# An eleventh expert tile is kept in h, the gathers read x, and the experts' sum is collected beside x

## What is computed

```python
for l in range(DEPTH):                                   # DEPTH = 2
    ...
    x = x + jnp.sum(g * br, axis=2) @ w_out[l]
    x = x + _cross_attention(_rms_norm(x, cross_norm_g[l]), ...)
    x = x + _hier_moe(_rms_norm(x, ffn_norm_g[l]), w_group[l], b_group[l], w_router[l],
                      b_router[l], w1[l], w3[l], w2[l])
return _rms_norm(x, final_norm_g)

# _hier_moe: 32 experts in 4 groups, each token goes to the best 2 of its best group
def expert_block(args):
    xb, e = args
    return (jax.nn.silu(xb @ w1[e]) * (xb @ w3[e])) @ w2[e]
```

## Time and profile before

| | |
|---|---|
| time, median of 3 runs | 1585.15 us (1585.04 to 1585.71) |
| span of the profiled execution | 1584.5 us (no other time is recorded for that execution) |
| TensorE busy | 1280.7 us, 81% |
| VectorE busy | 622.2 us, 39% |
| ScalarE busy | 301.9 us, 19% |
| DMA moved | 502.32 MB, mean 317 GB/s |
| chain that ended last | TensorE 51%, DMA 41% |

### The profile page before, as it was taken

One profiled execution on the slowest core, in us unless ns is written; L12 is line 12 of the kernel. 1 busy time (PEld: TensorE's weight loads), 2 busy tenths in 40 slices (PEclk: granted clock), 3 DMA queues, 4 the chain that ended last, 5 costly groups with the idle time before them and its releaser, 6 DMA issues.

```text
span 1584.5 us, 18206 instructions
## 1 busy us (share of the span) xinstructions
PE 1280.7 (81%) x7334; PEld 674.6 (43%) x7334; DVE 622.2 (39%) x1218; ACT 301.9 (19%) x748; POOL 24.0 (2%) x38
## 2 busy tenths in 40 slices
PE   8999999998666567677699999999986666756656
PEld 7986544463212123233279865445632211312211
DVE  5777676353122121121165866663531121121121
ACT  2235422251000001000032453212400000000002
POOL 2000000000000000000000000000000000000000
PEclk9999999999878888788899999999998777888788
DMA  9742236969999999999986323477899999999996
GB/s 295 237 161 80 80 107 241 347 252 393 421 421 422 421 413 421 421 421 421 420 290 192 122 80 108 170 264 285 300 420 422 421 421 420 420 421 420 422 421 266
DMA packets 125080, 502.32 MB, mean 317 GB/s; under 512 B 9408, under 2 KB 46336, under 8 KB 77888
## 3 DMA queue, kind: packets, MB, share of 16 engines
q1 hardware_dynamic: 121728, 494.41, 79.4%
q10 hardware_dynamic: 1888, 4.19, 0.7%
q0 software_dynamic: 1376, 2.48, 0.7%
HBM read 500.00 MB, written 1.05 MB: 316 GB/s over the span
## 4 chain that ended last, share of the span: by engine, by line
PE 51%; DMA 41%; SPq 2%; DVE 2%; ACT 2%; issue 2%; ACTq 0%; DVEq 0%
DMA ring<-in_w_dram 40%; PE banks L2453 9%; PE banks L2751 7%; PE banks L2358 6%; PE banks L2819 5%; PE banks L2508 5%; PE banks L2913 3%; PE banks L2351 3%; PE banks L2250 2%; SPq L745 2%; PE banks L2618 1%; PE banks L2651 1%; DMA ring<-in_w_in_dram 1%; PE banks L2897 1%; PE banks L2951 1%
## 5 line engine op out<-in xcount | busy, mean ns | idle before, releaser
L2751 PE MATMUL banks<-ring,v 128*32 128x512 f32 x1888 | 296.4, 759 | 182.5 <-DMA ring<-in_w_dram 173.5
L2751 PEld LDWEIGHTS banks<-ring,v 128*32 128x32 f32 x1888 | 79.5, 135 | 385.5 <-issue 382.2
L2819 PE MATMUL banks<-ring,probT 128*32 128x512 f32 x960 | 144.2, 724 | 80.3 <-DMA ring<-in_w_dram 74.1
L2819 PEld LDWEIGHTS banks<-ring,probT 128*32 128x32 f32 x960 | 37.8, 129 | 170.3 <-issue 161.3
L1846 DVE COPY q<-banks 128x512 f32<-128x512 f32 x16 | 11.1, 692 | 237.5 <-PE banks L2819 206.3
L1842 DVE TENSOR_TENSOR q<-banks,q 128x512 f32<-128x512 f32 x16 | 11.1, 692 | 209.7 <-PE banks L2751 209.7
L1835 DVE TENSOR_SCALAR q<-q 128x512 f32<-128x512 f32 x16 | 6.8, 427 | 165.3 <-ACT q L1079 165.3
L2692 PE MATMUL banks<-v,h 128*128 128x128 f32 x448 | 57.7, 291 | 14.3 <-issue 14.3
L2692 PEld LDWEIGHTS banks<-v,h 128*128 128x128 f32 x448 | 55.0, 204 | 26.8 <-issue 26.8
L2453 PE MATMUL banks<-ring,hT 128*128 128x512 f32 x144 | 64.9, 594 | 0.0
L1074 ACT ACTIVATE v<-banks,fcol 128x128 f32<-128x128 f32 x56 | 16.0, 368 | 256.2 <-PE banks L2692 256.2
(11 more groups left out here) (420 smaller groups left out, 1862.6 us busy)
## 6 DMA issues: line engine op xcount, KB each, us to landing
ring<-in_w_dram SPq DMA_DIRECT2D x348, 1024.0 KB, 19.4
ring<-in_w_in_dram SPq DMA_DIRECT2D x52, 1024.0 KB, 7.7
ring<-in_w_branch_dram SPq DMA_DIRECT2D x12, 1024.0 KB, 6.1
ring<-in_w_out_dram SPq DMA_DIRECT2D x8, 1024.0 KB, 12.6
ring<-in_w_dram SPq DMA_DIRECT2D x16, 512.0 KB, 14.3
shared<-in_w_dram SPq DMA_DIRECT2D x6, 1024.0 KB, 6.4
k<-in_w_dram SPq DMA_DIRECT2D x4, 1024.0 KB, 7.2
hT<-in_w_dram SPq DMA_DIRECT2D x4, 1024.0 KB, 11.6
```

What stands on the lines that cost most here:

```text
L2751: last = nc.tensor.matmul(bank[2 + m][e * CAP:(e + 1) * CAP, :], xt[:, k, e * CAP:(e + 1) * CAP], ws[e](r), start=k == 0, stop=k == KD - 1)
L2819: last = nc.tensor.matmul(bank[6 + half][e * CAP:(e + 1) * CAP, :], hiddenT[:, k, e * CAP:(e + 1) * CAP], ws[e](2 * r + half), start=k == ...
```

## The change

1. `EXTRA` becomes 11 and `AHEAD` gets tile 18 (`2 * KD + 2`, the third `w2` tile of round 0): it lies in `h`, loaded by SP after the first eight ring tiles, behind a wait on the last part of the third branch. The numbering of the turns moves by one; the length of a layer stays 252 turns, with 6 empty ones at its end in place of 5.
2. ACT's four writes of `h` are gone. Every gather reads `x` itself; its columns are taken with a step of 4 elements (16 bytes). The factor 1/rms is in the selection: `pick_tokens` makes it with four `tensor_scalar` of 128 x 32 for each half of the tokens, compare and multiply.
3. The rounds' results are collected in `h` (`added_up`): a copy in round 0, additions in rounds 1 to 6. In round 7 `fold_sums` adds `h` to `x` with four instructions of 128 x 512 before the wait for the second half of `w2`, and that round's own results are added to `x`.
4. The squares before the cross attention write their junk into `v0`, with a wait on earlier squares where it is used again.

```diff
-EXTRA = 10
-AHEAD = [KD + i for i in range(7)] + [2 * KD, 2 * KD + 1, KD - 1]
+EXTRA = 11
+AHEAD = [KD + i for i in range(7)] + [2 * KD, 2 * KD + 1, KD - 1, 2 * KD + 2]
...
-        h_rows = h[:, :, :].rearrange("p t (g r f) -> p t g r f", f=P, r=ROWS_IN)
+        x_rows = x[:, :, :].rearrange("p t (g f r) -> p t g r f", f=P, r=ROWS_IN)
+        added_up = h
...
-                    probT[:, 0, :, :, :].rearrange("p a b n -> p (a b n)"), v1[:, 1, :]]]
+                    probT[:, 0, :, :, :].rearrange("p a b n -> p (a b n)"), v1[:, 1, :]],
+                   [h[:, :, :].rearrange("p t n -> p (t n)")]]
...
                 quad_turns(0, in_ring[:RING - 4])
+                wait_free(sp, l, BRANCHES_AT[2] + 3)
+                load_beside(l, 10)
                 sp.wait_ge(mix_turned, l * 4 + 4)
...
-                half_squares(l, 1, 0, 0, h[:, 0, 0:512])
-                half_squares(l, 1, 0, 1, h[:, 0, 512:1024])
+                half_squares(l, 1, 0, 0, v0[:, 0, :])
+                half_squares(l, 1, 0, 1, v0[:, 1, :])
                 half_copies(l, 1, 0, 0)
                 half_copies(l, 1, 0, 1)
-                half_squares(l, 1, 1, 0, h[:, 1, 0:512])
+                act.wait_ge(squared, l * SQUARES + SQUARES_AT[1] + 2)
+                half_squares(l, 1, 1, 0, v0[:, 0, :])
...
-                for t in range(TT):
-                    act.wait_ge(root_step, root_done(l, 2, t))
-                    for half in range(2):
-                        cols = slice(half * 512, half * 512 + 512)
-                        last = nc.scalar.activation(h[:, t, cols].rearrange("p (r f) -> p f r", r=ROWS_IN),
-                                                    x[:, t, cols].rearrange("p (f r) -> p f r", r=ROWS_IN),
-                                                    ACT.Copy, scale=rstd(t))
-                    last.then_inc(h_made, 1)
...
+            def pick_tokens(t, col):
+                for e in range(QUAD):
+                    last = nc.vector.tensor_scalar(sel[:, t, e * CAP:(e + 1) * CAP], places, place[:, t, bass.ds(col + e, 1)],
+                                                   rstd(t), ALU.is_equal, ALU.mult)
+                return last
+
+            def fold_sums(l):
+                dve.wait_ge(main_r["added"], ((l + 1) * QUADS - 1) * 4 + 1)
+                for c in range(4):
+                    t, cols = c // 2, slice(c % 2 * 512, c % 2 * 512 + 512)
+                    nc.vector.tensor_tensor(x[:, t, cols], x[:, t, cols], added_up[:, t, cols], ALU.add).then_inc(folded, 1)
...
+                if ends is not None:
+                    fold_sums(ends)
                 wait_w2b(dve)
                 nc.vector.tensor_copy(yexp[:, 512:1024], bank[7][:, :]).then_inc(S["y_dve"], 1)
...
-                    xs = x[:, t, half * 512:half * 512 + 512]
-                    nc.vector.tensor_tensor(xs, xs, bank[(5, 2)[c % 2] if ends is None else END_BANKS[c]][:, :], ALU.add).then_inc(S["added"], 1)
+                    cols = slice(half * 512, half * 512 + 512)
+                    to, part = (added_up, bank[(5, 2)[c % 2]]) if ends is None else (x, bank[END_BANKS[c]])
+                    if ends is not None:
+                        dve.wait_ge(folded, ends * 4 + c + 1)
+                    if first:
+                        last = nc.vector.tensor_copy(to[:, t, cols], part[:, :])
+                    else:
+                        last = nc.vector.tensor_tensor(to[:, t, cols], to[:, t, cols], part[:, :], ALU.add)
+                    last.then_inc(S["added"], 1)
...
-                pe.wait_ge(h_made, l * 2 + 1)
-                pe.wait_ge(first_sel, l + 1)
+                pe.wait_ge(first_chosen, l * 3 + 2)
                 first_gather(0, (0, 1))
```

More of the change, by code:

```diff
@@ L421, in bass_hybrid_encoder @@
         xq_in, xo_in, xq_made, xcol_in = sem("xq_in"), sem("xo_in"), sem("xq_made"), sem("xcol_in")
-        max_raw, h_made = sem("max_raw"), sem("h_made")
+        max_raw, folded = sem("max_raw"), sem("folded")
         qx_copied = sem("qx_copied")
@@ L428, in bass_hybrid_encoder @@
         first_gathered, first_xt = sem("first_gathered"), sem("first_xt")
-        first_placed, first_sel = sem("first_placed"), sem("first_sel")
+        first_chosen = sem("first_chosen")
         stored, passed = sem("stored"), sem("passed")
@@ L1214, in _ @@
                 exps(X0 + 1)
-                half_squares(l, 1, 1, 1, h[:, 1, 512:1024])
+                half_squares(l, 1, 1, 1, v0[:, 1, :])
                 half_copies(l, 1, 1, 1)
@@ L1224, in _ @@
                 act.wait_ge(hT_dve, l * COPIES_DVE + COPIES_AT[2])
+                act.wait_ge(squared, l * SQUARES + SQUARES_AT[1] + 4)
                 half_squares(l, 2, 0, 0, v0[:, 0, :])
@@ L1804, in gained_xt, with experts_round, make_sel @@
                 return nc.vector.tensor_tensor(xt[:, 4:8, :], bank[1][:, :].rearrange("p (c n) -> p c n", c=4), cols, ALU.mult)
-            def experts_round(S, wait_w3, wait_w2b, rd, q, look, fresh, ends=None):
-                def make_sel(cols):
-                    nc.vector.tensor_tensor(
-                        sel.rearrange("p t (e s) -> p t e s", e=QUAD),
-                        places.rearrange("p (a b s) -> p a b s", a=1, b=1).broadcast_to([P, TT, QUAD, CAP]),
-                        place[:, :, cols].rearrange("p t (e s) -> p t e s", s=1).broadcast_to([P, TT, QUAD, CAP]),
-                        ALU.is_equal).then_inc(S["sel_made"], 1)
+            def pick_tokens(t, col):
[8 more added lines that the diff above has]
+                    nc.vector.tensor_tensor(x[:, t, cols], x[:, t, cols], added_up[:, t, cols], ALU.add).then_inc(folded, 1)
+            def experts_round(S, wait_w3, wait_w2b, rd, q, look, fresh, ends=None, first=False):
+                def make_sel(col):
+                    for t in range(TT):
+                        last = pick_tokens(t, col)
+                    last.then_inc(S["sel_made"], 1)
                 def copy_xt(k):
@@ L1818, in experts_round @@
                 if fresh:
-                    make_sel(bass.ds(q * QUAD, QUAD))
+                    make_sel(q * QUAD)
                     copy_xt(rd + 1)
                 if look:
-                    make_sel(bass.ds(q * QUAD + QUAD, QUAD))
+                    make_sel(q * QUAD + QUAD)
                 here = bass.ds(q * QUAD, QUAD)
@@ L2112, in first_place @@
                     nc.vector.scalar_tensor_tensor(place[:, t, 0:N_EXPERTS], bank[RANK_BANKS[t]][:, 0:32], 1.0,
-                                                   chosen[:, t, :], ALU.add, ALU.mult).then_inc(first_placed, 1)
+                                                   chosen[:, t, :], ALU.add, ALU.mult).then_inc(first_chosen, 1)
                 def make_first_sel(t):
-                    dve.wait_ge(first_placed, l * TT + t + 1)
-                    return nc.vector.tensor_tensor(
-                        sel[:, t, :].rearrange("p (e s) -> p e s", e=QUAD),
-                        places.rearrange("p (b s) -> p b s", b=1).broadcast_to([P, QUAD, CAP]),
-                        place[:, t, 0:QUAD].rearrange("p (e s) -> p e s", s=1).broadcast_to([P, QUAD, CAP]),
-                        ALU.is_equal)
+                    dve.wait_ge(first_chosen, l * 3 + 2 * t + 1)
+                    return pick_tokens(t, 0)
                 pick(1, 0)
@@ L2129, in _ @@
                 pick(1, 5)
-                make_first_sel(0).then_inc(first_sel, 1)
+                make_first_sel(0).then_inc(first_chosen, 1)
                 pick(1, 6)
@@ L2192, in _ @@
                                   lambda e: e.wait_ge(slot_free, done_at(l, q, PER_QUAD - 1)),
-                                  l * QUADS + q, q, looks_ahead(q), q == CHECK, l if q == QUADS - 1 else None)
+                                  l * QUADS + q, q, looks_ahead(q), q == CHECK, l if q == QUADS - 1 else None, q == 0)
                 end_root(l, 0)
```

5 lines of the change are left out of this document (2 added, 3 removed).

## The result

The changed kernel takes 1592.0 us (median of 6 runs, 1590.54 to 1595.74) against 1585.96 us before (6 runs on the same chip, 1585.04 to 1588.3): ratio 1.0033, 95% interval 1.0024 to 1.0043. It is 5.2 us slower; 1580.2 us was forecast. The profiled execution took 1592.32 us around a span of 1590.5 us.

A forecast was written before the change was run, and what follows sets the result against it. Bytes still to be moved once the DMA engines fill up were taken to bound each layer's experts. Span 1584.5 - 5.0 for the tile, all else 0 or hidden, is 1579.5, plus 0.65: 1580.2 us; range 1579.2 to 1584.2 us.

The forecast's parts named there:

- The tile in h: One tile of 1.049 MB a layer leaves the full stretch: 2.50 us a layer, -5.0 us for two.
- The border of the layers: Among layer 1's six first loads, the third now waits for the last pair of w2 tiles: cost 0.
- ScalarE: Loses four instructions of 1158 ns, 4.6 us a layer, that ran beside VectorE's choosing: no gain.
- the fold: Four additions of 0.69 us, 2.8 us, before the copy at 799.84 us, hidden in DVE's 14.89 us idle.
- VectorE's selections: First selections take 0.78 us for 0.28, +0.50 each, at 0.195 an operation; +1.0 us on PE's first expert matmul.
- The +1.0 us of DVE disappears in both: PE's later start, from the first selections, costs nothing in either layer because queued loads cover it.
- The room: Delay of PE that queued loads hide: 4.1 and 4.2 us at 1163 to 1168 us, 9.3 us in layer 0.
- a rival: Stepped loads are slow, up to 0.10 us a pair: 1583.5 us, at worst 1585.9; chance 0.20.
- TensorE, the gathers: Loading columns at a step of 16 bytes adds 0 to 0.12 us a pair; bounds 0 and 0.10.
- the bound of 0.10: Upper price of the step on a gather's pair, from ACT's scattered copy; 6.4 us over 64 pairs.
- the third: Slower: stepped gathers empty layer 1's queue; needs 0.127 us on a pair, 1591.8 us at 0.18; chance 0.08.
- signs: Gather's 32 pairs 3.8 or up to 7 us; wrong if GB/s below 400 after 1160 us or layer 0's end unmoved.

The follow-up runs named there:

- run 9: The changed kernel with contiguous columns in all gathers and each first selection as one compare and one multiply: ratio 0.9976, 1582.12 us.
- run 5: The changed kernel with contiguous columns in all gathers and selections in one instruction without 1/rms: 5112.79 us with repeated rounds; layer 1 begins at 807.15 us.
- run 1: The changed kernel with all gathers taking contiguous columns: ratio 0.9991, 1585.88 us.
- run 7: The changed kernel with contiguous columns in the first gathers alone: 5115.47 us with repeated rounds; layer 1 begins at 808.47 us.
- run 4: The changed kernel with a step of two in all rounds, w1 and w3 tiles in runs of 4 KB: ratio 1.0079.
- run 8: The changed kernel with contiguous columns in round 4's own gather alone: ratio 1.0021.
- run 2: The kernel before with the step alone, ACT writing h plainly and gathers reading it at a step of four: ratio 1.0044.
- run 3: The changed kernel without the eleventh tile beside the ring: ratio 1.0055.

## Why the prediction was wrong

Two steps failed. The gathers were put at no cost ("I take the nearest row, the PE one: 0") and cost 0.12 us a pair. And PE's delay was to disappear in the room of the queue, where the first loads that wait for PE had almost none.

**The tile in h** did what was said: its load is issued between the eight ring tiles and `k` (296.99 us, 0.47 us on the queue), at no cost, and it came out of the full stretch. Its worth was put at 5.0 us and measured 3.5 and 3.6. Whether the other 1.4 us are lost or noise isn't clear, and where they went isn't shown; it would fit that the DMA engines aren't full right behind the start, where this tile would have been loaded (296 GB/s at 360 to 364 us in the kernel before), but no run was made for that.

**The border of the layers, ScalarE and the fold**: nothing speaks against cost 0. The fold ran in VectorE's idle time (2.49 us from 786.44 us on). None of them was tried alone.

**VectorE's selections.** The size was put at 0.50 us each and was 0.63 (0.91 against 0.28): a small operation with two pointer operands takes 0.23 us, and the row of 0.195 us was of another one. The step that failed is "The +1.0 us of DVE disappears in both". It was paid for, by run 9 with 2.4 us over two layers, 2.4 either way (run 5: 1.22 in layer 0).

**The room.** That is the failed step behind the last one. Room was read at the tiles issued from 1163 us on, 4.1 us, and at those from 382 us on. But the first loads that wait for PE are the pieces behind the first `w1` tiles, and in front of those there was next to none: 360 to 364 us of the kernel before stand at share 0.91 and 296 GB/s, a window that the prediction didn't read. It wrote that these pieces have "less in front of them" and counted up to 2.4 us there for a rival only (24 pairs; the trace has 20 in front of the first `w1` tiles and 12 more in front of the second part). A delay of PE's start is lost there nearly in full: the second part of `w1` starts 3.56 us later than in run 1 (368.53 for 364.97), and layer 1 begins 3.22 us later. The room at the later place was there in layer 0, put at 9.3 us: the look-ahead gather's 3.9 us disappeared in it when the start was on time (run 7). Layer 1's 4.1 us were too many. With round 0 alone at a step of two `w2` starts 4.9 us later than before there (1164.63 for 1159.72), 4.4 of them since the layer began, and 1.9 were lost: some 2.5 us of room, an estimate from single executions.

**TensorE, the gathers**: the failed term with the largest price. A pair was put at +0 and costs +0.12 us (7.73 us for 32 against 3.84); outside even the bound of 0.10, which came from ACT's factor of 1.83: here it is 2.0. The nearest row, the hidden rows at 8 bytes, was near in bytes but not in what happens: run 4 shows a load at a step of 8 bytes at 196 ns, the change one at 16 bytes at 329 ns. This is the rule of the Trainium skill that the prediction weighed and left out of the sum (Advanced Engine Details and Errata, section SBUF Cachelines: lines of 16 bytes, two hits wanted on each). Here the trace agrees with both of its halves: two hits on a line are free or nearly so (16 matmuls in 2.13 against 2.03 us), one hit costs double.

**The rivals.** The case that came is the third, which had a chance of 0.08, and it came at its threshold: a pace of 0.24 us, for which it gave next to no loss. From its own working 64 x 0.122 + 1.0 = 8.8 us of delay in front of layer 1's `w2` were to be expected; measured by the chain are 1171.46 - 1159.72 = 11.7 us, less the 3.2 us by which layer 1 began late, 8.5. It would have made of that 1580.2 + 4.7 = 1584.9 us. The rest of the way to 1592.0 is the pieces in layer 0 (3.1 us), the tile's missing 1.4 us, round 4's own gather, which the prediction never named (0 to 1.9 us), and the time around the span, 1.8 us and not 0.65. That last one isn't the change's: the kernel before has 1.8 us too (1586.04 around 1584.2 beside run 1), and 0.65 was the median of some executions over the span of another. 3.1 + 1.4 + 1.2 and 0 to 1.9 are 5.7 to 7.6 us where 7.1 are missing; how much is lost in layer 1's pieces no run tells by itself.

**The sum by the runs**: tile -3.6, selections +2.4, step +6.7 to +7.0, together +5.5 to +5.8 against a measured +5.2 us. The single terms carry 2 to 2.7 us either way, so that they meet so closely is in part luck.

What it had named as signs was right: 7.7 us for the gather's 32 pairs, GB/s below 400 after 1160 us (366 from 1165 to 1190 us), and layer 0's last tiles not earlier.

## What to carry to other kernels

Room in a queue is to be read at the first load that waits for the delayed engine, and in a window of a few microseconds around it, not where the queue has filled again: between the two windows that were read lay 4 us at share 0.91 (296 GB/s), and there next to nothing was free. A strided stationary operand is to be priced by how many elements it takes of 16 bytes (here four or two: 192 and 196 ns a load, one: 329 ns), and a price that no row covers, here of 64 pairs in a row, wants a wide bound. A buffer won by giving up a contiguous copy is only worth its tile if the copy's layout was worth less.

## What the runs showed of the hardware that was not expected

**TensorE's clock fell at the stepped gather.** Windows of the changed kernel at the first gathers of both layers (PEclk is the third number from the end):

```profile
358.00:360.00 2.00, 2.00 (x10) 2.00 (x10) 1.56 (x10) 0.11 (x1) 0.00 (x0) 0.50 0.99 389
1140.00:1142.00 2.00, 2.00 (x11) 2.00 (x10) 1.60 (x9) 0.54 (x4) 0.00 (x0) 0.50 1.00 389
```

and of the kernel before in layer 0:

```profile
358.00:360.00 2.00, 2.00 (x24) 0.65 (x20) 0.00 (x0) 0.00 (x0) 0.00 (x0) 1.00 1.01 421
```

The granted clock is 0.50, the level of 1.2 GHz, while the 16 stepped loads and their matmuls ran. With a step of four it fell at six of the eight first gathers (both layers here and in run 8, layer 1 alone in run 2, layer 0 alone in run 3). With contiguous columns or a step of two it stayed at 1.00, the level of 2.4 GHz, at those of nine kernels; but in run 7, whose first gather is contiguous, it fell in layer 1 before that gather began (0.72 at 1132 to 1134 us, 0.50 behind it). So that the step brings the clock down is likely and not shown. The fall's own price here is small as far as rows tell: the 32 `w1` matmuls behind took 3.97 us in layer 0 and 3.64 where the clock was back, so 0.3 us. It isn't always: the second fall in run 8 made 96 matmuls 1.6 us longer.

**A stepped load doesn't follow the clock, a contiguous one does.** Round 4's own gather in layer 0, with a window inside it, first of the kernel before, then of the changed one:

```profile
574.19 5.88 PE L2692 MATMUL banks<-v,h 128*128 128x128 f32 x32 [7.33 <-issue]
576.00:578.00 2.00, 2.00 (x12) 2.00 (x11) 0.00 (x0) 0.00 (x0) 0.00 (x0) 0.50 1.00 414
```

```profile
575.89 7.73 PE L2707 MATMUL banks<-v,x 128*128 128x128 f32 x32 [7.27 <-issue]
576.00:578.00 2.00, 2.00 (x9) 2.00 (x10) 0.00 (x0) 0.00 (x0) 0.00 (x0) 0.50 1.02 426
```

The contiguous gather took 3.84 us where the granted clock was 1.00 and takes 5.88 where it is partly 0.50; its loads go from 192 to 333 ns (medians of the look-ahead gather, and from 574 to 578 us). The stepped one takes 7.73 us in both places, its loads 330 and 329 ns. So at 0.50, the level of 1.2 GHz, the step costs a load nothing, and its price is the one of full clock only.

**Runs of 4 KB are slower than those of 8 KB** at a full queue: 413 to 414 against 421 GB/s (run 4). The engines' share is full in both cases, so such a loss shows only in the GB/s of long windows.

**A multiply of 128 x 128 in SBUF costs no more than the compare** (0.29 and 0.28 us), while four of 128 x 32 with a pointer each take 0.91 us: fewer and wider instructions, even with a wait between the two, were 0.3 us faster at each selection.
